# Experts' input gathered in plain fp32 from the normalized rows, and five more weight units loaded ahead

## The reference

```python
g_idx = argmax(t @ w_group + b_group)                  # one of 4 groups per row
top_w, top_i = top_k(softmax(e_logits[g_idx]), 2)      # 2 of its 4 experts
combine = one_hot(g_idx) * within * g_w                # [256, 16]
for e in range(16):
    hdn = silu(t @ w_gate[e]) * (t @ w_up[e])          # [1024 x 512] each
    y = y + combine[:, e:e+1] * (hdn @ w_down[e])      # [512 x 1024]
h = layer_norm(ALPHA * h + y)
```

## Time and profile before

| what | us |
|---|---|
| median of 3 runs | 1746.06 (1745.6 to 1746.08) |
| the profiled execution | 1750.48 |
| its span, first to last instruction | 1748.7 |
| TensorE busy in the span | 1693.2 (97%) |
| VectorE, ScalarE, GpSimd busy | 879.4, 671.7, 101.6 |
| experts' stage of layer 0, first gathering to last scatter | 136.69 to 362.71 |
| experts' stage of layer 1 | 508.47 to about 739.6 |

### The profile page before, as it was taken

One profiled execution on the slowest core, in us unless ns is written; L12 is line 12 of the kernel. 1 busy time (PEld: TensorE's weight loads), 2 busy tenths in 40 slices (PEclk: granted clock), 3 DMA queues, 4 the chain that ended last, 5 costly groups with the idle time before them and its releaser, 6 DMA issues.

```text
span 1748.7 us, 20129 instructions
## 1 busy us (share of the span) xinstructions
PE 1693.2 (97%) x8422; PEld 1232.7 (70%) x8422; DVE 879.4 (50%) x1158; ACT 671.7 (38%) x920; POOL 101.6 (6%) x97
## 2 busy tenths in 40 slices
PE   9999999889999979989999999999999999999998
PEld 7774443369864434378888878888888888788886
DVE  5572121167761211275456676455655457875445
ACT  6442111146621111154433754444344336644432
POOL 1020000010000000000003002000200021020000
PEclk9999999989999999999999999999999999999999
DMA  9559999994369999955556426555655556255551
GB/s 349 181 212 360 421 421 421 421 316 147 143 274 412 420 420 421 403 174 193 180 181 206 165 94 223 178 187 172 226 182 191 180 163 229 97 193 193 179 171 59
DMA packets 142624, 426.50 MB, mean 244 GB/s; under 512 B 7592, under 2 KB 20144, under 8 KB 117952
## 3 DMA queue, kind: packets, MB, share of 16 engines
q1 hardware_dynamic: 136720, 407.00, 63.2%
q0 software_dynamic: 5808, 18.17, 3.3%
HBM read 424.08 MB, written 1.06 MB: 243 GB/s over the span
## 4 chain that ended last, share of the span: by engine, by line
PE 84%; DMA 6%; DVE 6%; ACT 4%; issue 1%; POOL 0%; SPq 0%; DVEq 0%
PE ps L569 18%; PE ps L561 17%; PE ps L564 17%; PE ps L1756 15%; DMA whole<-in_moe_w_up 5%; PE ps L691 2%; PE ps L553 2%; PE ps L554 2%; PE ps L1709 2%; PE ps L1821 2%; ACT mx_S L2893 2%; DMA whole<-in_moe_w_down 1%; DVE Wlo L497 1%; DVE mx_S L3102 1%; PE ps L2619 1%; PE ps L671 1%
## 5 line engine op out<-in xcount | busy, mean ns | idle before, releaser
L497 DVE TENSOR_TENSOR Wlo<-raw,Whi 128x2048 fp32r<-128x2048 f32 (+3 forms) x199 | 435.8, 2197 | 351.0 <-ACT Whi L486 350.7
L486 ACT ACTIVATE Whi<-raw 128x2048 fp32r<-128x2048 f32 (+3 forms) x205 | 375.8, 1842 | 375.8 <-PE ps L569 371.3
L569 PE MATMUL ps<-Whi,XTl 128*128 128x512 f32 (+2 forms) x1208 | 445.8, 385 | 0.0
L561 PE MATMUL ps<-Whi,XTh 128*128 128x512 f32 (+2 forms) x1048 | 408.5, 390 | 2.6 <-DVE mx_wT L3111 2.4
L564 PE MATMUL ps<-Wlo,XTh 128*128 128x512 f32 (+2 forms) x1048 | 403.8, 385 | 0.0
L569 PEld LDWEIGHTS ps<-Whi,XTl 128*128 128x128 f32 x1208 | 226.2, 190 | 44.0
L1756 PE MATMUL ps<-whole,p_XG 128*64 128x512 f32 (+2 forms) x992 | 232.1, 603 | 11.8 <-DMA whole<-in_moe_w_up 9.0
L561 PEld LDWEIGHTS ps<-Whi,XTh 128*128 128x128 f32 x1048 | 197.8, 189 | 43.1 <-issue 3.1
L564 PEld LDWEIGHTS ps<-Wlo,XTh 128*128 128x128 f32 x1048 | 197.7, 189 | 37.3 <-issue 0.2
L1756 PEld LDWEIGHTS ps<-whole,p_XG 128*64 128x64 f32 (+2 forms) x992 | 74.6, 138 | 147.1 <-issue 145.8
L1933 DVE TENSOR_TENSOR Ygl<-ps,Ygh 128x512 fp32r<-128x512 f32 x32 | 22.1, 691 | 235.7 <-ACT Ygh L1888 235.7
(11 more groups left out here) (363 smaller groups left out, 1734.1 us busy)
## 6 DMA issues: line engine op xcount, KB each, us to landing
whole<-in_moe_w_up SPq DMA_DIRECT2D x64, 1024.0 KB, 13.6
whole<-in_moe_w_down SPq DMA_DIRECT2D x64, 1024.0 KB, 14.7
whole<-in_moe_w_gate SPq DMA_DIRECT2D x60, 1024.0 KB, 13.4
raw<-in_ffn_gate SPq DMA_DIRECT2D x40, 1024.0 KB, 5.1
raw<-in_ffn_up SPq DMA_DIRECT2D x40, 1024.0 KB, 5.1
raw<-in_ffn_down SPq DMA_DIRECT2D x40, 1024.0 KB, 5.0
raw<-in_w_in SPq DMA_DIRECT2D x18, 1024.0 KB, 6.2
raw<-in_a_w_in SPq DMA_DIRECT2D x10, 1024.0 KB, 15.1
```

Source lines behind the costliest of these rows:

```text
L486: act.activation(Whi[:, hi_at[i], 0:m * n], raw[:, raw_at[i], 0:m * n], ACT.Copy).then_inc(w_rounded, tick(w_rounded, "rounded", i))
L497: dve.tensor_tensor(Wlo[:, raw_at[i], 0:m * n], raw[:, raw_at[i], 0:m * n], h.bitcast(f32), ALU.subtract).then_inc(w_rest, tick(w_rest, "r ...
L561: pe.matmul(o, xh(k, t), h[:, q, :], start=k == first, stop=False)
L569: x = pe.matmul(o, xl(k, t), h[:, q, :], start=False, stop=k == end)
```

## The change

Slots: five buffers of 8192 bytes inside `big_o` (offsets 0, 16384, 32768, 8192, 24576) take units of each layer's first pairs, its "guests". A guest is loaded as soon as the mixer's data in that place is dead. The first three buffers then stay in the ring of slots (14 in place of 11), the other two serve once a layer. `pXG` moves to `XT_o + 8192` and `big_o + 8192`, `Ygh`, `Ygl` and `lgT` move too. The gathering reads x itself. Its two splits are gone, and the first gathering is issued in two halves, two banks before the first chunk and two after it.

```diff
+    whole_more = [at_(f"whole{i}", [128, 2048], f32, big_o + o) for i, o in enumerate((0, 16384, 32768, 8192, 24576))]
...
-    w_landed = [semaphore(f"w_landed{i}") for i in range(NR + NS)]
+    w_landed = [semaphore(f"w_landed{i}") for i in range(NR + NS + 5)]
...
+    def guests(l):
+        js = jobs["first pair", l] + [jobs["first up", l]]
+        return {js[0][1]: (0, "scored", l), js[1][0]: (4, "weighed", l), js[1][1]: (2, "gated all", l),
+                js[2][0]: (3, "gated all", l), js[2][1]: (1, "gated all", l)}
+
+    guest = {**guests(0), **guests(1)}
+
     def place_units():
 
-        held_by, raw_at, hi_at, raw_next, hi_next = [-1] * (NR + NS), {}, {}, {}, {}
+        MORE = NR + NS
+        held_by, raw_at, hi_at, raw_next, hi_next = [-1] * (MORE + 5), {}, {}, {}, {}
+        entered = 0
...
-            a = oldest(range(NR) if i not in whole or near else range(NR + NS))
+            entered = entered + (i in guest and guest[i][0] < 3) if i in whole else 0
+            if i in guest:
+                a = MORE + guest[i][0]
+            else:
+                a = oldest(range(NR) if i not in whole or near else [a for a in range(MORE + 3) if a < MORE or entered == 3])
...
     def load_units(sp, a, b):
...
-            ring = whole_ if i in whole else raw
-            sp.dma_start(ring[:, raw_at[i], 0:m * n].rearrange("p (t n) -> p t n", n=n), ap).then_inc(
+            if i in guest:
+                sp.wait_ge(*on(*guest[i][1:]))
+            to = whole_unit(i) if i in whole else raw[:, raw_at[i], 0:m * n].rearrange("p (t n) -> p t n", n=n)
+            sp.dma_start(to, ap).then_inc(
...
+                if (c, g) == (3, 1):
+                    point["scored", 0] = point["weighed", 0] = point["update", 3, 1]
...
+            point["gated all", 0] = point["gated", g, t]
...
-    pXn = (at_("p_Xnh", [128, 2, 1024], f32r, big_o + 16384), at_("p_Xnl", [128, 2, 1024], f32r, big_o + 24576))
-    pXG = at_("p_XG", [128, 2, 8, 256], f32, big_o)
+    pXG = [at_(f"p_XG{i}", [128, 8, 256], f32, o) for i, o in enumerate((XT_o + 8192, big_o + 8192))]
...
-    def pair_split_act(act, l, v, t):
-        act.wait_ge(*on("x", v, t))
-        act.activation(pXn[0][:, t, :], X[:, t, :], ACT.Copy).then_inc(act_done, tick(act_done, "xn_hi", l, t))
-
-    def pair_split_dve(dve, l, t):
-        dve.wait_ge(*on("xn_hi", l, t))
-        dve.tensor_tensor(pXn[1][:, t, :], X[:, t, :], pXn[0][:, t, :].bitcast(f32), ALU.subtract).then_inc(
-            dve_done, tick(dve_done, "xn", l))
...
-    def pair_gather_pe(pe, l, z):
+    def pair_gather_pe(pe, l, z, groups=range(4)):
         n = MAIN[l].name
         pe.wait_ge(*on(n, "P", 2 * z + 1))
-        pe.wait_ge(*on("xn", l))
-        for kg in range(4):
+        for kg in groups:
             b = bank(pe, n, "xg", z, kg)
             for q in range(2):
                 k = 2 * kg + q
                 for t in range(2):
-                    for a in pXn:
-                        x = pe.matmul(PS[b][:, q * 256:(q + 1) * 256], a[:, t, k * 128:(k + 1) * 128],
-                                      pP[:, t, 256 * z:256 * z + 256],
-                                      start=t == 0 and a is pXn[0], stop=t == 1 and a is pXn[1])
+                    pe.wait_ge(*on("x", 2 * l + 1, t))
+                    x = pe.matmul(PS[b][:, q * 256:(q + 1) * 256], X[:, t, k * 128:(k + 1) * 128],
+                                  pP[:, t, 256 * z:256 * z + 256].bitcast(f32), start=t == 0, stop=t == 1)
...
-        pair_gather_pe(pe, l, 0)
+        pair_gather_pe(pe, l, 0, (0, 1))
...
             for k, ids in enumerate(jobs["first pair", l]):
+                if k == 1:
+                    pair_gather_pe(pe, l, 0, (2, 3))
                 got(0, k)
...
+                if (h, t) == (7, 1):
+                    point["scored", 1] = point["score", 7, 1]
...
+            if h == 7:
+                for e in ("weighed", "gated all"):
+                    point[e, 1] = point["value", 7]
```

More of the change, by code:

```diff
@@ L455, in whole_unit @@
     def whole_unit(i):
-        return whole_[:, raw_at[i], :].rearrange("p (t n) -> p t n", n=512)
+        a = raw_at[i] - NR - NS
+        v = whole_more[a][:, :] if a >= 0 else whole_[:, raw_at[i], :]
+        return v.rearrange("p (t n) -> p t n", n=512)
     def groups(name, skew=False, hold=0):
@@ L1425, in router_dve @@
             dve_done, tick(dve_done, "router", l))
-    Ygh = at_("Ygh", [128, 1024], f32r, big_o + 32768)
-    Ygl = at_("Ygl", [128, 1024], f32r, big_o + 36864)
-    lgT = at_("lgT", [40, 256], f32, big_o + 32768)
+    Ygh = at_("Ygh", [128, 1024], f32r, big_o + 24576)
+    Ygl = at_("Ygl", [128, 1024], f32r, big_o + 28672)
+    lgT = at_("lgT", [40, 256], f32, big_o + 40960)
     fgh = at_("fgh", [128, 2, 512], f32r, sh_o)
@@ L1556, in pair_route_act @@
         ex = o4[:, 1, :, :]
-        pair_split_act(act, l, v, 0)
         first_half_act(act, l, 0)
         x_turn_act(act, v, 1)
-        pair_split_act(act, l, v, 1)
         round_units(act, last_unit(v) + NS)
@@ L1569, in pair_route_dve @@
     def pair_route_dve(dve, l, v):
-        pair_split_dve(dve, l, 0)
         x_turn_dve(dve, v, 1)
@@ L1608, in pair_route_dve @@
         dve.tensor_tensor(g_(5), g_(4), g_(3), ALU.subtract).then_inc(dve_done, tick(dve_done, "top_gap", l))
-        pair_split_dve(dve, l, 1)
         dve.wait_ge(*on("ranks", l))
@@ L1719, in pair_gather_act @@
                 act.wait_ge(*on("used", jobs["pup", l, 2 * z - 3][-1][-1]))
-            act.activation(pXG[:, z % 2, 2 * kg:2 * kg + 2, :], PS[where[n]][:, :].rearrange("p (k n) -> p k n", n=256),
+            act.activation(pXG[z % 2][:, 2 * kg:2 * kg + 2, :], PS[where[n]][:, :].rearrange("p (k n) -> p k n", n=256),
                            ACT.Copy).then_inc(act_done, tick(act_done, "in", *n))
@@ L1770, in side @@
             c = 128 * (p % 2) + w * s
-            return pXG[:, p // 2 % 2, 4 * u + q, c:c + w]
+            return pXG[p // 2 % 2][:, 4 * u + q, c:c + w]
         return side
```

## The result

The changed kernel takes 1753.07 us (median of 9 runs, 1749.83 to 1757.96) against 1745.65 us before on the same chip (9 runs, 1744.37 to 1749.72). The ratio is 1.0035, with a 95% interval from 1.0024 to 1.0046: slower by some 6.1 us, 4 to 8. The forecast was 3.1 us slower and 1749.2 us; the time lies inside the range, on the side named as the likelier one. The profiled execution took 1753.12 us (span 1751.3), so it is a typical run, while that of before was 4.8 us above its median.

A forecast was written before the change was run, and what follows sets the result against it. Loading was taken to cost 30.2 us in the experts' stages, with TensorE setting the time elsewhere. +25.3 + 1.8 - 0.4 - 12.5 - 11.1 = +3.1 us on the median of 1746.06 gave 1749.2, 8-in-10 range 1742.5 to 1755.5.

The forecast's parts named there:

- Dearer gathering, +25.3: Eight expert gatherings, plain fp32 instead of fp32r matmuls: 3.16 us more each, paid in full, +25.3 us (16.4 to 30.5).
- Loading waits, -12.5 and -11.1: TensorE's waits for units in the experts' stages: all 12.5 us go in layer 0; layer 1 gains 11.1 of 17.7.
- Layer 0, about 1 us longer: Sign to look for in the changed profile: layer 0's experts' stage about 1 us longer.
- Layer 1, 2.5 us longer: Sign to look for in the changed profile: layer 1's experts' stage about 2.5 us longer.
- the 2.0: Layer 1, behind the remaining wait of about 4.6 us: 2.0 us lost to low clock, taken between 1.7 and 2.8.
- Bare copy, +1.8: Behind each layer's first chunk, ScalarE's copy of the gathering's last bank lies bare: 0.9 us a layer, +1.8 (0 to 2.4).
- Splits, -0.4: Splits left out: in layer 1 the rest of XT starts earlier on VectorE, -0.4 us; elsewhere 0.
- Difference of the profile put on the median: The predicted +3.1 us, worked out on the profiled execution (1750.48), was added to the median of 1746.06, giving 1749.2.
- The 4.5 us of lower clock booked as lost in layer 1: Two chunks behind layer 1's waits of 4.21 and 5.57 us, at clock 0.50, take 1.7 + 2.8 us more.
- Cheaper or dearer matmul: Rivals for the 128 gathering matmuls: 0.368 us each, 1740.3, chance 0.09; or 0.478 (or more bare copies), 1754.4, chance 0.10.
- Loading binds to the end: Rival, experts' stages: loading hides the gatherings and the five-unit lead, 12.4 us a layer, comes off; 1721, chance 0.01.
- Wait in layer 1 whole: Rival, layer 1's chunks behind 630: nothing comes off the 17.7 us; +11.1, 1760.3, chance 0.07.

The follow-up runs named there:

- the room alone: Changed kernel with gatherings of 32 matmuls on rounded x as before in number, type and length, five extra units kept; 1738.05 us, ratio 0.9944 to the kernel before.
- the late fetch: Kernel before with the next norm's 1 MB of weights fetched after each layer's last gathering, not at the layer's start; 1749.47 us, ratio 1.0013.
- kept awake: Changed kernel with 18 matmuls, overwritten afterwards, before the second down chunk of layer 1's four-expert group; 1752.35 us, ratio 1.0027 to the kernel before.
- first gathering whole: Changed kernel with each layer's first gathering whole in front of the first chunk; 1749.73 us, ratio 1.0015 to the kernel before.
- that with more on TensorE: Changed kernel with 16 extra plain fp32 matmuls before each of layer 0's second and third gatherings, results overwritten; 1766.67 us, ratio 1.0100 to the kernel before.
- the kernel before with more on TensorE: Kernel before with 16 extra plain fp32 matmuls before each of layer 0's second and third gatherings, results overwritten; 1755.04 us, ratio 1.0042.

## Why the prediction was right, and what was wrong in it

- *Dearer gathering, +25.3.* The size holds: 6.91 against 3.83 us is 3.08 each, 24.6 for eight (3.16 and 25.3 foretold). What failed is "a longer gathering is paid in full", taken as true of the kernel before: alone it costs 13.1 us, because 9 us of waits for units go with it, and of 13.8 us more on TensorE in layer 0 only 5.3 were paid there, but all 13.8 in the changed kernel.
- *Loading waits, -12.5 and -11.1.* The waits of layer 0 did go, but I booked them all to the five units. By the runs the room alone brings 9.8 us in both layers together (an estimated 2 to 3 more without the late fetch). The two errors are one: waits that either part alone would remove were booked once, to the room, and the gathering at its full price, and for the sum that is the same. It came out right because I had carried the stream through for both parts together, and not by luck in layer 0: its stage grew by 0.3 us though its gatherings cost 12.3 more and its bare copy 0.7, so 12.7 us of loss to loading went, where 12.5 were foretold. Parted, +25 and -24 would have misled: they are +13 and -10.
- *Layer 0, about 1 us longer.* 0.3.
- *Layer 1, 2.5 us longer.* 4.8. The gain of 11.1 was taken too high: by the same count (12.3 + 0.7 + 1.7 for the lower clock in the half gathering - 0.3 for the splits - 4.8) it was 9.6. The wait was 5.59, not 4.6: TensorE came when foretold (36.4 us from the first of the two requests, at 620.97, to the start of the wait, 36.2 foretold), but from the second request at 624.65 to the landing of the last unit it took 38.2 us, not 37.0; one unit on the way landed 3.63 us behind its predecessor. The same unit comes 3.6 to 3.9 us behind its predecessor in three profiles (the changed kernel, kept awake, first gathering whole), while the DMAs move about 420 GB/s. Behind the wait the clock cost 1.4, not 2.0; behind the same wait of 5.6 us it cost 2.6 in the kernel with the first gathering whole and 2.1 in that with more on TensorE, so the 2.0 was a fair middle. And 1.7 us went into the half gathering at the lower clock, which no term had. 2.5 + 1.0 + 1.7 - 0.6 makes 4.6. The Trainium skill's rule (TensorE: Matmul & The Clock Gate, "HAM oscillation — how this bites in real kernels") agrees with the trace in direction; its price in this profile was 1.4 us.
- *Bare copy, +1.8.* 0.73 us of idle in layer 0 and 0.7 in layer 1, as foretold; the whole first gathering won 1.2 and 1.3 us. *Splits, -0.4.* From the start of x's last write to the first gathering of layer 1: 12.49 us before, 12.23 after.
- *Difference of the profile put on the median.* This step was loose. The profile of before held 45 us of lower clock, that of after 37, and behind the experts of layer 1, where it has 8 us less of lower clock, the changed kernel's profile is 2.5 us quicker. The two profiles differ by 2.6 us in time and the medians by 7.4. I added stage differences to the median, which was right. The 4.5 us of lower clock booked as lost in layer 1 are no accident of one run. In the kernel before with more on TensorE the same two chunks take 8.92 and 6.52 us, where the kernel before has 8.87 and 6.48:

```profile
639.32 8.92 PE L1759 MATMUL ps<-whole,p_XG 128*32 128x512 f32 x40 [4.06 <-DMA whole<-in_moe_w_up]
664.14 6.52 PE L1759 MATMUL ps<-whole,p_hT 128*32 128x512 f32 x32 [5.59 <-DMA whole<-in_moe_w_down]
```

Every one of the five profiles with a wait of some 4 us at the first place shows the slow chunk behind it (8.8 to 10.1 us). Between the profiles of before and after it is the lower clock behind the experts' stages that differs most.
- *Rivals.* Cheaper or dearer matmul: 0.432 each, neither. Loading binds to the end: the after windows show TensorE full in layer 0; by the 358 GB/s of the Trainium skill (DMA: Bandwidth & Descriptors, "Where 436 GB/s comes from") it would have, but over the two long stretches every kernel here moved more, from 390 to 421. Wait in layer 1 whole: half of it stayed, 5.6 of 12.6.

What stays open: 0.9 us of the 6.1 are in neither stage (within the interval), and why one unit landed late, in three kernels at the same place.

## What to carry to other kernels

When the paces of the loading and of an engine lie within a few per cent, the price of work on one and of waits on the other can't be booked apart. Cut a long steady stretch as one window and see which of the two is full, before and after. A start in loading is worth only what the ring can hold: three places that stayed were worth 13 us here, and five used once nothing. And an added megabyte in a stretch where the DMAs are full put off the later units by 2.5 us here, the time of its own transfer, though another queue issued it; what that costs in the end was 3.3 us in layer 0 and nothing in layer 1.

## What the runs showed that I had not expected

- The clock fell to 0.51 in layer 1's first gathering, from 508.9 to 512.3, behind a wait of 0.38 us, in four of five profiles of kernels that have that gathering in two parts and in none of eight that have it whole. TensorE's work ahead of it is alike in all. The link is an observation, not a mechanism.
- With five guests' places used once the queue idled 14 us, and the kernel was 6 us slower than the one with the long gathering and none of the five (some 2.5 of it may be the first gathering's two parts).
- The kernel before spread over 1744.4 to 1752.8 us across sessions; its longer runs have the lower mean clock (of 29 runs in one session the five fastest stand at 0.990 to 0.991, the five slowest at 0.986 to 0.988), so runs agree only as far as their stretches of lower clock do.
